# Hybrid decoder step on one core: the first projection of the first 384 tokens taken from x before its norm, and the work around it in another order

## The chip, the core and the metric

The kernel runs on one core of one Trainium2 chip. The core has TensorE (PE in the profile; PEld is its weight load), VectorE (DVE), ScalarE (ACT), GpSimd (POOL) and SyncE (SP), which run side by side and wait for each other through semaphores; SP and ACT also start DMA transfers, each on a queue of its own. The metric is the device time of one execution in microseconds, as the median of several.

## The reference, cut to what matters

One decoder layer for 1024 prompt tokens and 8 x 4 sample tokens (1056 columns together). What the change touches is its very beginning:

```
h = RMSNorm(x)                        # x * rstd(token) * norm1(channel)
proj = h @ w_in                       # z, xBC, dt, u, q, k, v and three gates
u -> S5 branch: a complex diagonal scan over steps, y = Re(C h) + D u
gates = sigmoid(proj[gate columns])   # 3 x 1024 columns
```

rstd is one number for each token, so that x*norm1 @ w, multiplied with rstd afterwards, is the same as h @ w. After this come three mixers, their merging by the gates, an output projection, and the SwiGLU feed-forward part, which are not changed.

## The kernel before, in words

Activations lie transposed: 128 channels on the partitions, tokens along the columns. `HH` and `HL` (8 tiles k of 1056 columns) hold the high and the low half of h in a reduced float format; `WH` and `WL` the same of a weight unit (128 output columns of W, 8 blocks k of 128x128). A product is three matmuls for each k: WH by HL, WL by HH, WH by HH (`mm3`). Tokens are handled in three chunks (`CHUNKS`): 384, 384 and 288 columns, called chunk 0, 1 and 2.

**The u stage.** Weight units 0 to 3 give u. Units 0 and 1 lie in `WRAW`/`WH`/`WL`, 2 and 3 in `WXR`/`WXH`/`WXL`. `u_pair(j, n)` makes units j and j+1 for chunk n, k by k, so that it can follow the arrival of the halves of h; its order is (0,0), (2,0), (0,1), (2,1), (0,2), (2,2), 48 matmuls each. Before a chunk's h can be made, its squares are summed (squares on ACT and DVE, sums of them over k on DVE), the sum over channels taken by `x_sums_pe`, root on ACT (`x_root_act`), reciprocal on DVE (`x_recip_dve`), and the result spread over the partitions by `x_spread_pe`. Then for each k DVE writes x*norm1*rstd (line 702), ACT copies its high half to HH (line 714), and DVE subtracts that to give HL (line 691). For chunk 0 all of this lies ahead of the first `mm3`. ACT casts the first weights to WH by halves of 512 columns (`high_half`), POOL subtracts to give WL (`split_halves`, `split_apart`). ACT copies u from PSUM to `UF` (`evict_u`) and stores it; SP loads it back in another layout (`U`, lines 1063 and 1067) once all four stores have landed.

**The gates.** From unit 4 on PE makes twelve gate units (`gate(g, chunks)`), each with the accumulators `acc[0..2]` for the three chunks. A chunk of tile `no` starts when `acc_free[n]` says that all `no` earlier tiles of that chunk have been evicted; gate 0 is tile 4. ACT evicts each chunk with a tanh into the one buffer `GT` and stores it (line 2330); the next gate's first tanh waits for that store. Between gates PE does small S5 products: `taps(q)` needs `W_re` and `W_im`, which DVE makes from POOL's tables out of six operations of 2048 columns after its last HL (semaphore `w_ok`); `stt_rows(q)` transposes them, ACT evicting; `step_sums` needs U.

All orders are written by hand, one program for each engine. An instruction that waits holds everything behind it on its engine.

Of the kernel before, what the change touches and what calls it, by code (L numbers as in the profile page):

```python
# [9 lines left out]
F32 = mybir.dt.float32  # L10
# [6 lines left out]
P = 128  # L17
# [139 lines left out]
def build(nc, io):  # L157
# [255 lines left out]
    s_xc = [dma_sem("x_chunk1_first"), dma_sem("x_chunk1_last"), dma_sem("x_chunk2")]  # L413
# [6 lines left out]
    first_high, half_ok = sem("first_weights_high"), sem("first_weights_half_split")  # L420
    s_rawx = [dma_sem(f"weights_second_pair{i}") for i in range(2)]
# [47 lines left out]
    s_fst = [Count(s_xc[0], 64), Count(s_xc[1], 64), Count(s_xc[2], 128), Count(s_scv, 16)]  # L469
    s_fop = [Count(s_x[k], 32) for k in range(7)]  # L470
    wt_ok, wh_ok, wl_ok = Count(den_ok, 1), Count(us_ok, 1), Count(ar_ok, 1)
    pd, ar_used, dr = Count(bias_mm, 2), Count(step_ok, 1), Count(sem("quadrant_made"), 0)
    dd, si_ok = Count(den_inv, 1), Count(mag_ok, 1)
    ss_ok, sh_ok, sl_ok = Count(hf_done, 48), Count(h_hi, 48), Count(h_lo, 48)
    fm_ok, fs_ok, fh_ok, fl_ok = Count(sem("ffn_ready"), 0), Count(sem("ffn_sum"), 0), Count(sin_ok, 1), Count(w_ok, 1)
# [3 lines left out]
    h_lo_pool = sem("h_low_by_pool")  # L479
# [110 lines left out]
    def u_bank(j, n):  # L590

        return bank[((0, 1, 2, 3), (4, 6, 7, 0), (1, 2, 3, 4))[n][j]]

    FIRST_SQUARES, FIRST_ADDED = KD // 2, KD + 1
    Y_SQUARES, Y_ADDED = FIRST_SQUARES + 2 * KD, FIRST_ADDED + 2 * KD

    def x_square_at(n, k):

        if n == 0 and k >= 4:
            return ACC[:, 384 * (k - 4):384 * (k - 3)] if k < 6 else HF[k - 6]  # L600
        return SQ[:, k % 4, 0:CHUNKS[n][1]]
# [5 lines left out]
    def x_spread_at(n):  # L607

        return bank[(4, 7, 5)[n]]

    def x_full(i):

        return bank[5 + i % 2] if i < KD else HF[i % 2]

    def x_loaded(n, k):

        return s_x[k] if n == 0 else s_xc[k // 4] if n == 1 else s_xc[2]

    def x_first_square(eng, k):

        eng.wait_ge(x_loaded(0, k), 16)
        if k % 2 == 0:
            nc.scalar.activation(x_square_at(0, k), X0[:, k, 0:384], ACT.Square).then_inc(pq_done, 1)
        else:
            nc.vector.tensor_tensor(x_square_at(0, k), X0[:, k, 0:384], X0[:, k, 0:384], ALU.mult).then_inc(pq_used, 1)

    def x_squares_act(n, ks):
        c0, w = CHUNKS[n]
        base = FIRST_ADDED + KD * (n - 1)
        for k in ks:  # L630
            nc.scalar.wait_ge(x_loaded(n, k), (16, 64, 128)[n])
            if k >= 4 or n == 2:
                nc.scalar.wait_ge(pq_used, base + k - 3)
            nc.scalar.activation(x_square_at(n, k), X0[:, k, c0:c0 + w], ACT.Square).then_inc(pq_done, 1)

    def x_add_dve(n, ks):
        dve = nc.vector
        c0, w = CHUNKS[n]
        for k in ks:
            i = FIRST_ADDED + KD * (n - 1) + k  # L640
            dve.wait_ge(pq_done, FIRST_SQUARES + KD * (n - 1) + k + 1)
            if k == 0:
                dve.tensor_copy(ACC[:, c0:c0 + w], x_square_at(n, k)).then_inc(pq_used, 1)
            else:
                dve.wait_ge(pq_used, i)
                dve.tensor_tensor(ACC[:, c0:c0 + w], ACC[:, c0:c0 + w], x_square_at(n, k), ALU.add).then_inc(pq_used, 1)

    def x_first_sums_pe():

        for k, added in ((1, 2), (3, 4), (7, FIRST_ADDED)):  # L650
            nc.tensor.wait_ge(pq_used, added)
            for j in range(3):
                last = nc.tensor.matmul(x_sums_at(0)[:, j:j + 1], x_square_at(0, k)[:, P * j:P * j + P], prm("ones", 0, 1),
# [40 lines left out]
    def x_split_dve(i0, i1):  # L694
        dve = nc.vector
        for i in range(i0, i1):
# [7 lines left out]
            if k >= 1:  # L704
                x_low_dve(i - 1)
# [3104 lines left out]
```

## Time and profile before

| | us |
|---|---|
| median of 3 runs (1685.58 to 1688.41) | 1686.39 |
| span of the profiled execution | 1684.5 |
| PE busy in it | 1654.0 |
| DVE, POOL, ACT busy | 966.9, 791.2, 556.0 |

The times of runs contain some 2 us ahead of and behind the span. The profile lists work by engine, the line in the kernel and the tiles that an instruction writes and reads (out<-in), with its start and duration. "idle before <-" is how long the engine had stood still and what ended that. The busy share of PE counts matmuls that overlap, so how fast it goes is read from the distance between starts.

### The profile page before, as it was taken

The page shows a single profiled execution, that of the slowest core. Times are in us where ns is not written, and L with a number is a line of the kernel's source. Part 1 is how long each engine was busy: PE and PEld are TensorE (multiplying, and loading weights), DVE is VectorE, ACT ScalarE, POOL GpSimd, SP SyncE. Part 2 cuts the span into 40 slices and gives each one's busy share as a digit, 9 for nine tenths or more (in the row PEclk, how much of TensorE's full clock was granted, in tenths as well). Part 3 has the DMA queues.
Part 4 walks back from the last instruction along what each step waited for, and adds up shares of the span by engine and source line. Part 5 has one row for each costly group of instructions (what it writes and reads, how often), then busy time and mean ns, then how long its engine had stood idle before and what let it go on. Part 6 is the DMA issues. An engine that isn't in the chain of part 4 may idle for free. (4 is left out here: it accounts for less than half of the span.)

```text
span 1684.5 us, 30884 instructions
## 1 busy us (share of the span) xinstructions
PE 1654.0 (98%) x12241; PEld 1604.7 (95%) x12241; DVE 966.9 (57%) x1642; ACT 556.0 (33%) x1240; POOL 791.2 (47%) x756
## 2 busy tenths in 40 slices
PE   7999999999999999999999999999999999999997
PEld 7999999999999998888899999999999999999997
DVE  6859811406634554778873289666665565744346
ACT  5332121342213332543411154443443333322233
POOL 5483122322221111141322325877777777787774
PEclk9999999999999999999999999999999999999998
DMA  5364363232233234434365431543433344966443
GB/s 209 84 127 133 104 203 98 89 92 91 87 93 103 89 130 134 161 115 140 126 218 191 152 126 42 180 162 145 151 141 141 141 167 165 367 224 267 162 187 103
DMA packets 95805, 245.85 MB, mean 146 GB/s; under 512 B 14369, under 2 KB 42273, under 8 KB 95417
## 3 DMA queue, kind: packets, MB, share of 16 engines
q1 hardware_dynamic: 73824, 174.48, 30.5%
q0 software_dynamic: 10256, 33.59, 6.7%
q10 hardware_dynamic: 11592, 35.96, 6.3%
q8 instruction: 90, 1.47, 0.4%
q14 instruction: 43, 0.34, 0.1%
HBM read 177.11 MB, written 66.65 MB: 145 GB/s over the span
## 5 line engine op out<-in xcount | busy, mean ns | idle before, releaser
L1642 PE MATMUL ps<-HL,WH 128*128 128x384 f32 (+1 forms) x1536 | 507.7, 331 | 4.4 <-DVE HL L691 1.8
L1643 PE MATMUL ps<-HH,WL 128*128 128x384 f32 (+1 forms) x1536 | 497.4, 324 | 0.0
L1644 PE MATMUL ps<-HH,WH 128*128 128x384 f32 (+1 forms) x1536 | 496.3, 323 | 0.0
L1642 PEld LDWEIGHTS ps<-HL,WH 128*128 128x128 f32 x1536 | 289.4, 188 | 15.6 <-issue 9.3
L1643 PEld LDWEIGHTS ps<-HH,WL 128*128 128x128 f32 x1536 | 289.7, 189 | 0.3
L1644 PEld LDWEIGHTS ps<-HH,WH 128*128 128x128 f32 x1536 | 289.6, 189 | 0.0
L1285 POOL TENSOR_TENSOR WL<-WRAW,WH 128x1024 fp32r<-128x1024 f32 x59 | 145.0, 2457 | 243.3 <-DMA WH<-in_w 243.3
L1282 POOL DMA_DIRECT2D WH<-in_w x59 | 34.6, 586 | 354.4 <-PE ps L1644 352.9
L2932 DVE TENSOR_TENSOR X<-X,ps 128x528 f32<-128x528 f32 (+2 forms) x170 | 107.9, 656 | 155.5 <-PE ps L2238 104.6
L2327 ACT ACTIVATE GT<-ps 128x384 f32<-128x384 f32 (+1 forms) x72 | 33.4, 465 | 215.5 <-PE ps L1644 183.5
L2932 DVE TENSOR_TENSOR RB<-RB,ps 128x528 f32<-128x528 f32 x60 | 42.1, 701 | 103.4 <-ACT RB L2847 85.9
L1310 POOL TENSOR_TENSOR WRAW<-WRAW 128x512 f32<-128x512 f32 (+2 forms) x72 | 91.8, 1275 | 9.9 <-DVE STG L2932 4.6
L1310 POOL TENSOR_TENSOR RAWB<-RAWB 128x512 f32<-128x512 f32 (+2 forms) x72 | 87.6, 1216 | 5.4
L2236 PE MATMUL ps<-HL,RINGB 128*128 128x264 f32 x272 | 77.4, 285 | 2.1 <-DVE GT L2932 2.1
L2237 PE MATMUL ps<-HH,RINGB 128*128 128x264 f32 x280 | 79.5, 284 | 0.0
L2238 PE MATMUL ps<-HH,RINGB 128*128 128x264 f32 x280 | 79.5, 284 | 0.0
L2236 PE MATMUL ps<-HL,WH 128*128 128x264 f32 x274 | 77.9, 284 | 0.3 <-issue 0.3
L2236 PE MATMUL ps<-HL,WL 128*128 128x264 f32 x270 | 76.6, 284 | 0.0
L2236 PE MATMUL ps<-SOP,RINGB 128*128 128x264 f32 x264 | 75.2, 285 | 0.0
L2237 PE MATMUL ps<-HH,WL 128*128 128x264 f32 x264 | 75.0, 284 | 0.0
L2238 PE MATMUL ps<-SOP,RINGB 128*128 128x264 f32 x264 | 74.9, 284 | 0.0
L2237 PE MATMUL ps<-SOP,RINGB 128*128 128x264 f32 x264 | 74.9, 284 | 0.0
(467 smaller groups left out, 4266.2 us busy)
## 6 DMA issues: line engine op xcount, KB each, us to landing
WRAW<-in_w SPq DMA_DIRECT2D x75, 512.0 KB, 3.4
ffn_scratch<-STG SPq DMA_DIRECT2D x70, 528.0 KB, 3.6
WH<-in_w POOLq DMA_DIRECT2D x62, 512.0 KB, 4.6
SOP<-ffn_scratch SPq DMA_DIRECT2D x36, 528.0 KB, 7.9
gate_scratch<-GT ACTq DMA_DIRECT2D x24, 528.0 KB, 3.2
PX<-gate_scratch ACTq DMA_DIRECT2D x22, 528.0 KB, 4.2
HL<-ffn_scratch SPq DMA_DIRECT2D x22, 528.0 KB, 10.4
RAWB<-in_w SPq DMA_DIRECT2D x10, 1024.0 KB, 6.2
```

The source lines that it names most:

```text
L1282: nc.gpsimd.dma_start(WH[:, slot, 0:wd], src[:, 0:wd]).then_inc(s_high[slot], 16)
L1285: nc.gpsimd.tensor_tensor(WL[:, slot, 0:wd], WRAW[:, slot, 0:wd], WH[:, slot, 0:wd].bitcast(F32), ALU.subtract).then_inc(split_ok, 1)
L1310: return nc.gpsimd.tensor_tensor(out, a, b, op)
L1642: nc.tensor.matmul(out, wh, rl, start=start, stop=False)
L1643: nc.tensor.matmul(out, wl, rh, start=False, stop=False)
L1644: return nc.tensor.matmul(out, wh, rh, start=False, stop=stop)
L2236: nc.tensor.matmul(out, wh, ml, start=product in FRESH and k == 0, stop=False, skip_group_check=True)
L2237: nc.tensor.matmul(out, wl, mh, start=False, stop=False, skip_group_check=True)
L2238: last = nc.tensor.matmul(out, wh, mh, start=False, stop=k == nk - 1, skip_group_check=True)
L2327: nc.scalar.activation(GT[:, c0:c0 + w], acc_of(no, n)[:, 0:w], ACT.Tanh, scale=0.5).then_inc(acc_free[n], 1)
L2932: return nc.vector.tensor_tensor(out, a, b, op)
```

## The change

- **Chunk 0 of u from x without its norm.** ACT writes HH for chunk 0 as the high half of x*norm1 (`x_plain_high_act`), DVE writes HL from that (`x_plain_low_dve`). PE starts `u_pair(0, 0)` from these, behind no sum of squares. rstd of chunk 0 is made later, put in `GT[:, 0:384]`, and DVE multiplies with it when it evicts u of chunk 0 (`evict_first_u_dve`, four of them, formerly ACT copies).
- **The normed h of chunk 0**, which the gates and all later products need, is made last: the order of chunks in `x_split_*` is 1, 2, 0. So PE does gate 0 as chunks 1, 2 and then 0.
- **No wide POOL work in the u stage.** The low halves of weight units 0 to 4 are made by DVE; POOL only counts them and does its S5 tables earlier. The split of unit 5 and later ones stay on POOL.
- **Loads.** Units 0 and 1 come as four half loads on ACT's queue right behind the parameters; SP loads x of chunk 0, units 2 and 3, and then the rest.
- **Squares.** Those of chunks 0 and 1 are added in wide DVE operations; the sum over channels of chunk 0 moves from ahead of the first matmul into `u_pair(0, 1)`, the bias products into `u_pair(2, 0)`.
- **Products with W later.** taps(0) and taps(1) stand behind chunks 0 and 1 of gate 1, formerly behind gate 0's first two chunks; stt_rows(0) and (1) behind chunk 0 of gate 2.
- **ACT** puts the evictions of u between the copies of the split; those of chunk 2 for j = 2 and 3 stand behind the last copy.

```diff
-        return bank[((0, 1, 2, 3), (4, 6, 7, 0), (1, 2, 3, 4))[n][j]]
+        return bank[((0, 1, 2, 3), (4, 5, 6, 7), (1, 2, 3, 4))[n][j]]
+    ROOT_ORDER = (1, 0, 2)
+    SPLIT_ORDER = (1, 2, 0)
+    def x_plain_high_act(k):
+        nc.scalar.wait_ge(s_x[k], 16)
...
+        nc.scalar.mul(HH[:, k, 0:384], X0[:, k, 0:384], prm("norm1", k, 1)).then_inc(xp_hi, 1)
+    def x_plain_low_dve(k):
+        dve.wait_ge(xp_hi, k + 1)
+        dve.scalar_tensor_tensor(HL[:, k, 0:384], X0[:, k, 0:384], prm("norm1", k, 1), HH[:, k, 0:384].bitcast(F32),
+                                 ALU.mult, ALU.subtract).then_inc(xp_lo, 1)
+    def x_root_copy_act():
+        nc.scalar.wait_ge(pn_rs, 2)
+        nc.scalar.copy(GT[:, 0:384], x_spread_at(0)[:, 0:384]).then_inc(r0_ok, 1)
+    def evict_first_u_dve(j):
+        dve.wait_ge(r0_ok, 1)
+        dve.wait_ge(acc_done[0], j + 1)
+        dve.tensor_tensor(as_steps(UF[:, j, :], 0, 3), as_blocks(u_bank(j, 0), 3), as_blocks(GT[:, 0:384], 3),
+                          ALU.mult).then_inc(acc_free[0], 1)
# PE, u stage
-        x_first_sums_pe()
-        bias_by_distance(0)
-        bias_by_distance(1)
-        x_spread_pe(0)
         u_pair(0, 0)
-        pe.wait_ge(bias_ev, 2)
-        u_pair(2, 0, {1: lambda: x_sums_pe(1), 3: lambda: x_spread_pe(1)})
-        u_pair(0, 1)
-        u_pair(2, 1, {1: lambda: x_sums_pe(2), 3: lambda: x_spread_pe(2)})
+        u_pair(2, 0, {1: lambda: bias_by_distance(0), 2: lambda: bias_by_distance(1), 3: lambda: x_sums_pe(1),
+                      5: lambda: x_spread_pe(1)})
+        u_pair(0, 1, {1: lambda: x_sums_pe(0), 5: lambda: x_spread_pe(0)})
+        u_pair(2, 1, {2: lambda: x_sums_pe(2), 4: lambda: x_spread_pe(2)})
         u_pair(0, 2)
         u_pair(2, 2)
# PE, gates
-        gate(0, [0, 1])
+        gate(0, [1, 2])
+        gate(0, [0], lambda n, k: pe.wait_ge(h_lo, 2 * KD + k + 1))
+        gate(1, [0, 1])
         taps(0)
-        gate(0, [2])
         taps(1)
-        gate(1, [0])
+        gate(1, [2])
         taps(2)
-        gate(1, [1])
         taps(3)
-        gate(1, [2])
+        gate(2, [0])
         stt_rows(0)
-        for n in range(3):
-            gate(2, [n])
-            stt_rows(n + 1)
+        stt_rows(1)
+        gate(2, [1])
+        stt_rows(2)
+        gate(2, [2])
+        stt_rows(3)
# ACT, behind chunk 0
+        evict_u(0, 1)
+        evict_u(1, 1)
+        x_root_act(2)
+        x_split_act(8, 12)
+        evict_u(2, 1)
+        x_split_act(12, 14)
+        evict_u(3, 1)
+        x_split_act(14, 18)
+        evict_u(0, 2)
+        x_split_act(18, 19)
+        high_weights(4)
+        x_split_act(19, 20)
+        evict_u(1, 2)
+        x_split_act(20, 22)
+        high_weights(5)
+        x_split_act(22, 24)
         for j in range(4):
-            evict_u(j, 2)
-            if j == 1:
-                high_weights(4)
-                high_weights(5)
+            if j >= 2:
+                evict_u(j, 2)
+            act.wait_ge(acc_free[0], j + 1)
             act.wait_ge(acc_free[2], j + 1)
             act.dma_start(uscr[j * P:(j + 1) * P, :], UF[:, j, :]).then_inc(s_ust, 16)
# DVE, behind chunk 1
+        x_split_dve(4, 8)
+        x_third_sum_dve()
+        for j in range(3):
+            evict_first_u_dve(j)
         x_recip_dve(2)
-        x_split_dve(16, 24)
+        evict_first_u_dve(3)
+        x_split_dve(8, 20)
+        dve.wait_ge(first_high, 7)
+        tt(high_low(4)[1], WRAW[:, 0, :], high_low(4)[0].bitcast(F32), ALU.subtract).then_inc(half_ok, 1)
+        x_split_dve(20, 24)
```

ACT from its first instruction on, before; the names are the tiles written and read (SP is the table of S5 parameters, SQ, ACC and HF take squares of x, X is x as loaded):

```order
L2332 DMA PRM<-in_params 128x428
L2334 ACT_TABLE_LOAD
L2334 ACTIVATE SP<-ZERO 128x1
L2336 ACTIVATE SP<-PRM 128x16
L2338 ACTIVATE SP<-SP 128x16
L623 ACTIVATE SQ<-X 128x384 x2
L623 ACTIVATE ACC<-X 128x384
L623 ACTIVATE HF<-X 128x384
L2410 ACT_TABLE_LOAD
L2410 ACTIVATE SP<-ZERO 128x1
L2355 CAST WH<-WRAW 128x512 x2
```

and in the changed kernel:

```order
L2368 DMA PRM<-in_params 128x428
L2372 DMA WRAW<-in_w 128x512 x4
L2374 ACT_TABLE_LOAD
L2374 ACTIVATE SP<-ZERO 128x1
L2376 ACTIVATE SP<-PRM 128x16
L634 ACTIVATE HH<-X,PRM 128x384
L2448 ACTIVATE SP<-SP 128x16
L2393 CAST WH<-WRAW 128x512 x2
L634 ACTIVATE HH<-X,PRM 128x384 x3
L2393 CAST WH<-WRAW 128x512 x2
```

Four loads stand ahead of the first table load, and the first HH stands where squares stood.

DVE from its first instruction on in the changed kernel (UF and GT hold squares here; before it began with squares of x too, and its first HL was its twelfth operation):

```order
L640 SCALAR_TENSOR_TENSOR HL<-X,PRM,HH 128x384
L2977 TENSOR_TENSOR WL<-WRAW,WH 128x512 x2
L640 SCALAR_TENSOR_TENSOR HL<-X,PRM,HH 128x384 x3
L2977 TENSOR_TENSOR WL<-WRAW,WH 128x512 x2
L640 SCALAR_TENSOR_TENSOR HL<-X,PRM,HH 128x384 x4
L2977 TENSOR_TENSOR WXL<-WXR,WXH 128x1024 x2
L3017 RECIPROCAL SP<-SP 128x16
L651 TENSOR_TENSOR UF<-X 128x768
L677 TENSOR_TENSOR GT<-X 128x768
```

The weights' low halves, which were POOL's, stand between the low halves of x.

ACT at the end of the u stage, before (UF takes u, of which the 128x2x8x16 and 128x32 are chunk 2; WH of units 4 and 5):

```order
L714 CAST HH<-HF 128x288 x8
L2398 COPY UF<-ps 128x3x8x16 x2
L2398 COPY UF<-ps 128x2x8x16
L2400 COPY UF<-ps 128x32
L2453 DMA u_scratch<-UF 128x1056
L2398 COPY UF<-ps 128x2x8x16
L2400 COPY UF<-ps 128x32
L2348 CAST WH<-WRAW 128x1024 x2
L2453 DMA u_scratch<-UF 128x1056
```

and in the changed kernel:

```order
L2436 COPY UF<-ps 128x2x8x16
L2438 COPY UF<-ps 128x32
L779 CAST HH<-HF 128x384 x2
L2386 CAST WH<-WRAW 128x1024
L779 CAST HH<-HF 128x384 x2
L2496 DMA u_scratch<-UF 128x1056 x2
L2436 COPY UF<-ps 128x2x8x16
L2438 COPY UF<-ps 128x32
L2496 DMA u_scratch<-UF 128x1056
```

The stores of u and the evictions of its last two tiles stand behind the last copies of chunk 0's split, which come after those of chunk 2.

## Rows read from the trace of the kernel before

**Rows 1.** The page: the span, and PE's busy time, share and instructions.
```profile
span 1684.5 us, 30884 instructions
PE 1654.0 (98%) x12241; PEld 1604.7 (95%) x12241; DVE 966.9 (57%) x1642; ACT 556.0 (33%) x1240; POOL 791.2 (47%) x756
```
**Rows 2.** Waits of PE in the first 120 us: us in total, times, longest.
```profile
PE ps L653 <- DVE SQ L2932: 6.2, 1, 6.2
PE ps L1642 <- DVE HL L691: 1.8, 1, 1.8
```
**Rows 3.** Busy time of PE in stretches of the u stage (x matmuls), clock, DMA, GB/s.
```profile
17.30:21.00 3.70, 3.70 (x12) 1.00 1.08 368
21.00:27.30 6.30, 6.30 (x37) 1.00 0.83 315
```
**Rows 4.** Timeline of PE: start, us; where the u pairs and gate 0 begin.
```profile
17.30 0.69 PE L1642 MATMUL ps<-HL,WH 128*128 128x384 f32 x1 [1.82 <-DVE HL L691]
...
27.51 0.34 PE L1642 MATMUL ps<-HL,WXH 128*128 128x384 f32 x1
...
37.71 0.34 PE L1642 MATMUL ps<-HL,WH 128*128 128x384 f32 x1
...
46.11 0.34 PE L1642 MATMUL ps<-HL,WXH 128*128 128x384 f32 x1
...
56.12 0.29 PE L1642 MATMUL ps<-HL,WH 128*128 128x288 f32 x1
...
69.16 0.41 PE L1642 MATMUL ps<-HL,WH 128*128 128x384 f32 x1
```
**Rows 5.** Timeline of the start: parameters' arrival on ACT, DMA in one microsecond, bias products.
```profile
4.22 0.22 ACT L2336 ACTIVATE SP<-PRM 128x16 f32<-128x16 f32 x1 [1.38 <-DMA PRM<-in_params]
...
5.00:6.00 1.00, 0.00 (x0) 0.00 (x0) 0.77 (x2) 0.89 (x3) 0.83 (x3) 1.00 1.06 381
...
11.86 1.05 PE L1745 MATMUL ps<-HOT,RTAB 33*8 33x264 f32 x4
```
**Rows 6.** Timelines of ACT and DVE: weight casts, and h of chunk 1.
```profile
13.47 1.12 ACT L2355 CAST WH<-WRAW 128x512 fp32r<-128x512 f32 x2
...
36.75 0.61 DVE L702 SCALAR_TENSOR_TENSOR HF<-X,PRM,ps 128x384 f32<-128x384 f32 x1
37.28 0.56 DVE L691 TENSOR_TENSOR HL<-HF,HH 128x384 fp32r<-128x384 f32 x1
37.94 0.61 DVE L702 SCALAR_TENSOR_TENSOR HF<-X,PRM,ps 128x384 f32<-128x384 f32 x1
```
**Rows 7.** Timeline of ACT: eviction and store of u, tanh of gate 0's first chunk.
```profile
62.29 0.37 ACT L2398 COPY UF<-ps 128x256 f32<-128x256 f32 x1 [2.10 <-PE ps L1644]
62.56 0.19 ACT L2400 COPY UF<-ps 128x32 f32<-128x32 f32 x1
62.78 0.34 ACTq L2453 DMA_DIRECT2D u_scratch<-UF  x1
...
73.65 0.49 ACT L2327 ACTIVATE GT<-ps 128x384 f32<-128x384 f32 x1 [1.99 <-PE ps L1644]
```
**Rows 8.** Timelines of DVE (products for W) and of POOL (split of unit 4).
```profile
64.36 2.29 DVE L2932 TENSOR_TENSOR W_re<-W_re,KTS 128x2048 f32<-128x2048 f32 x1
66.69 4.36 DVE L2932 TENSOR_TENSOR W_im<-PWD,BC 128x2048 f32<-128x2048 f32 x1
...
75.48 2.29 DVE L2932 TENSOR_TENSOR W_im<-W_im,KTS 128x2048 f32<-128x2048 f32 x1
...
64.66 4.24 POOL L1487 TENSOR_TENSOR WL<-WRAW,WH 128x1024 fp32r<-128x1024 f32 x1 [9.78 <-ACT WH L2348]
```
**Rows 9.** Timelines of SP and ACT: U's first loads, gate 1's tanh, unit 7's cast.
```profile
76.56 9.19 SPq L1063 DMA_DIRECT2D U<-u_scratch  x8
...
97.51 0.87 ACT L2327 ACTIVATE GT<-ps 128x384 f32<-128x384 f32 x2 [12.35 <-DMA gate_scratch<-GT]
...
101.10 1.05 ACT L2348 CAST WH<-WRAW 128x1024 fp32r<-128x1024 f32 x1 [0.53 <-DMA WRAW<-in_w]
```

More of the change, by code:

```diff
@@ new lines, in x_first_squares_act, with x_first_rest_dve, x_first_add_dve @@
+    def x_first_squares_act(ks):
+        for k in ks:
+            nc.scalar.activation(SQ0[:, k, :], X0[:, k, 0:384], ACT.Square).then_inc(pq_done, 1)
+    def x_first_rest_dve():
+        dve, rest = nc.vector, slice(FIRST_BY_ACT, KD)
+        dve.tensor_tensor(SQ0[:, rest], X0[:, rest, 0:384], X0[:, rest, 0:384], ALU.mult).then_inc(x0_add, 1)
+    def x_first_add_dve(i):
+        dve = nc.vector
+        if i == 0:
+            dve.wait_ge(pq_done, FIRST_BY_ACT)
+        dve.wait_ge(x0_add, i + 1)
+        if i < 2:
+            n = 4 >> i
+            dve.tensor_tensor(SQ0[:, 0:n], SQ0[:, 0:n], SQ0[:, n:2 * n], ALU.add).then_inc(x0_add, 1)
@@ L648, in x_first_sums_pe, with x_second_sum_dve @@
[L648 to L653, printed above, removed]
-                                        start=(k == 1 and j == 0), stop=k == KD - 1, skip_group_check=True)
-        last.then_inc(pn_sum, 1)
-    def x_sums_pe(n):
-        nc.tensor.wait_ge(pq_used, FIRST_ADDED + KD * n)
+    def x_second_sum_dve():
+        dve, pairs = nc.vector, GT[:, 0:768].rearrange("p (k c) -> p k c", c=384)
+        dve.wait_ge(s_xc[1], 128)
+        dve.tensor_tensor(pairs, X0[:, 6:8, 384:768], X0[:, 6:8, 384:768], ALU.mult).then_inc(pq_used, 1)
+        dve.wait_ge(pq_done, FIRST_BY_ACT + 4)
+        dve.tensor_tensor(SQ[:, 0:2], SQ[:, 0:2], SQ[:, 2:4], ALU.add).then_inc(pq_used, 1)
+        dve.wait_ge(pq_used, 2)
+        dve.tensor_tensor(SQ[:, 0:2], SQ[:, 0:2], pairs, ALU.add).then_inc(pq_used, 1)
+        dve.wait_ge(pq_done, FIRST_BY_ACT + SECOND_BY_ACT)
+        dve.wait_ge(pq_used, 3)
+        dve.tensor_tensor(SQ[:, 0:2], SQ[:, 0:2], HF0[:], ALU.add).then_inc(pq_used, 1)
+        dve.wait_ge(pq_used, 4)
+        dve.tensor_tensor(ACC[:, 384:768], SQ[:, 0], SQ[:, 1], ALU.add).then_inc(pq_used, 1)
@@ L1541, in _ @@
                 split_apart(6)
-                s5_squarings(0)
                 s5_squarings(1)
@@ L1672, in unit, with gate @@
         def unit(u, slot, tiles):
-            pe.wait_ge(split_ok, u + 1)
+            pe.wait_ge(*((half_ok, 7) if isinstance(u, int) and u == UNIT0["gates1"] else (split_ok, u + 1)))
             for args, kw in tiles:
                 tile(args[0], slot, *args[1:], **kw)
-        def gate(g, chunks=range(3)):
+        def gate(g, chunks=range(3), before=None):
             u = (UNIT0["gates1"] + g) if g < 12 else (UNIT0["gates2"] + g - 12)
             no = (TILE0["gates1"] + g) if g < 12 else (TILE0["gates2"] + g - 12)
-            unit(u, u % 2, [((no, 0, KD, HH, HL), dict(chunks=chunks))])
+            unit(u, u % 2, [((no, 0, KD, HH, HL), dict(chunks=chunks, before=before))])
         def simple_loop(name, pairs, nk, RH, RL, skip=0, kbase=0, before=None):
@@ L2332, in _ @@
         act.dma_start(PRM[:, 0:NPAR_FIRST], io["params"][:, 0:NPAR_FIRST]).then_inc(s_par, 16)
+        for half in range(2):
+            c = slice(512 * half, 512 * half + 512)
+            for u in range(2):
+                act.dma_start(WRAW[:, u, c], io["w"][u][:, c]).then_inc(s_half0 if half == 0 else s_raw[u], 16)
         act.wait_ge(consts_ok, 1)
@@ L2494, in _ @@
         high_weights(7)
+        gate(2, [0])
         stt_rows(0)
-        for n in range(3):
-            gate(2, [n])
-            stt_rows(n + 1)
+        stt_rows(1)
+        gate(2, [1])
+        stt_rows(2)
+        gate(2, [2])
+        stt_rows(3)
         u_sample_copy()
```

288 lines of the change are left out of this document (140 added, 148 removed).

## The prediction, made before the changed kernel was run

> **What bounds the kernel now.** I read the page first: PE is busy for 1654.0 of 1684.5 us [rows 1], so only time in which PE stands still or runs slowly can be won. PE's waits give it: 6.2 us for the first squares and 1.8 us for the first low half HL are the largest of the first 120 us, and both lie ahead of the first projection matmul [rows 2]. That matmul starts at 17.30 us [rows 4]. What PE did before it is small sums and spreads. From there PE is never behind anything for long: 48 matmuls of 384 columns take 46.11 - 37.71 = 8.4 us, 0.175 us each, the 96 of 288 columns 69.16 - 56.12 = 13.0 us, 0.136 each [rows 4]. The first twelve are slow: 3.70 us for 12, then 6.30 us for 37, which is 0.31 and 0.17 us each, near 1.2 and then 2.4 GHz, though the granted clock reads 1.00 in both rows [rows 3]. So the prize is the start at 17.30, and whatever PE reaches earlier must be ready earlier too.
>
> **The new start.** Ahead of the first matmul now stand: half 0 of units 0 and 1 in WRAW, two casts on ACT, and on DVE the low half of x tile 0 and of both weight halves. The loads: the parameters (214 KB) came at 4.2 us, and DMA moves 381 KB in a microsecond [rows 5]. By the order of issue the second half-0 load has about 1.33 MB ahead of or in it (parameters, three tiles of x at 197 KB, two halves at 262 KB), 3.5 us at that rate; from a first byte at 2.5 us (4.2 less the time of parameters and two x tiles) and half a microsecond for the landing this is 6.5 us. The casts take 1.12 us for two [rows 6]. DVE's operation with 512 columns is bounded by 0.56 us for 384 [rows 6] and 2.29 for 2048 [rows 8], that is 0.16 us and 1.04 ns a column: 0.7 us, of which the second stands behind the second cast. 6.5 + 1.1 + 0.7 and some 0.3 for three handings-over: PE starts at 8.6 us, 8.7 earlier. The ends are 8.0 and 9.6. The Trainium skill ("DMA: Bandwidth & Descriptors", Arbitration) says that each DMA engine takes turns between its queues by packets. Then ACT's 0.74 MB would go at half the rate and land at 6.9 instead of 6.5 us; no row here shows two full queues side by side, and the sum goes without it.
>
> The twelve slow matmuls stay, since PE is as idle before as it was: no gain, no loss. Within u_pair(0,0) x tiles come every 0.5 us and ACT and DVE take 1.1 us for a tile's halves side by side; PE needs 1.05 us for a k at full speed, and 1.9 at first. I count no wait there. Units 2 and 3 need two DVE operations of 1.2 us (1024 columns), done at about 17 us, and PE is there at 18.8.
>
> **What moves behind the start.** The two bias products were hidden in PE's idle time (1.05 us at the slow rate [rows 5]); now they cost 0.5. So were the sums and spread of chunk 0: chunk 1's cost 37.71 - 27.51 - 8.4 = 1.8 us [rows 4], and chunk 0's will cost the same. Chunk 1's h: DVE makes a tile in 37.94 - 36.75 = 1.19 us [rows 6], PE uses one in 1.05. Before, PE never waited for it. Now the spread of chunk 1 ends only two k, 2.1 us, ahead of u_pair(0,1), and DVE needs 1.8 us from there to the first HL (twice 0.61 and 0.56). Between tiles 3 and 4 stands the reciprocal of chunk 0 (it waits for PE's sums and a root on ACT), and ahead of the copy of tile 7 stands ACT's copy of the spread of chunk 0, which is issued behind k = 5 on PE. Followed step by step, PE waits 0.2 to 0.3 us at k = 4 and 5 and 0.55 at k = 7: 0.85 together. The ends are 0.3 and 2. u_pair(2,1) and the pairs of chunk 2 I find just covered: DVE's last low half comes 8.5 us after the spread of chunk 2, PE wants it after 8.75.
> So gate 0 starts 8.7 - 0.5 - 1.8 - 0.85 = 5.55 us earlier, at 63.6.
>
> **The gates.** ACT's evictions of u, chunk 2, for j = 2 and 3 now stand behind its last copy for chunk 0. DVE splits chunk 0 after chunk 2, eight tiles of 1.19 us and unit 4's low half (1.2); its last tile but one is given to ACT about 2.3 us after PE's last u matmul. Behind that ACT does two stores and an eviction, a store, an eviction (0.34 and 0.56 us [rows 7]): the fourth is free some 4.5 us after gate 0's start. Gate 0's second chunk wants it after 4.2. **0.3 us**. Chunk 0 of gate 1 follows directly on chunk 0 of gate 0 with the same accumulator, and must wait for a tanh: 0.49 us [rows 7] and two handings-over. **0.75 us**; before, another chunk always lay between.
>
> W: DVE's six operations of 2.29 us make 13.75. DVE ends its splits some 5 us after gate 0's start, later by POOL's split of unit 5 (2.2 us, below) and of unit 6 within the products. w_ok is due at 63.6 + 5 + 2.2 - 1 + 13.75 + 2.2, about 85 us (it was 75.48 + 2.29 = 77.8 [rows 8]). PE is at taps(0) after 5 chunks of gates: 63.6 + 4 x 4.2 + 3.3 + 0.3 + 0.75 = 84.8. No wait of weight, by 0 to 1 us. Before, it was as near: w_ok at 77.8, with gate 0's two chunks done at 77.6. The order of the products a gate later costs nothing in itself: it is what PE needs as DVE's work ends later while PE comes earlier.
>
> At stt_rows(0) and (1), which now stand together behind gate 2's first chunk, the second pair of transposes waits for ACT to do the tanh and the first copy. **0.4 us**. Later stages depend on PE's own results (S5 rotations wait for the transposes) and move along. POOL's squarings come earlier, which shortens DVE's rotations, but PE did not wait for these: nothing.
>
> The sum: 5.55 - 0.3 - 0.75 - 0.4 = **4.1 us**. The profiled span of 1684.5 becomes 1680.4, and with the same 1.9 us around it the median becomes **1682.3 us**.
>
> **A rule against it.** With POOL's split of unit 4 asked for at 64.66 us, DVE's running operation took 2.29 us and its next one 4.36, and POOL's own 4.24 [rows 8]: one went wholly ahead of the other, each losing some 2.1 us. The Trainium skill ("SBUF — State Buffer", Who interferes with whom) says that a DVE instruction with two inputs in SBUF and a GpSimd one that reads SBUF share a port pair as an exclusive lock. The trace agrees. Unit 5's split remains on POOL and becomes ready when DVE is about to start its last multiplication for chunk 0, which has two SBUF inputs now (X and GT, formerly PSUM). By my walk DVE starts that one 0.1 us ahead of POOL. If POOL is first, ACT's last copy comes 2.2 us later and so do the evictions behind it.
>
> **Rivals.**
> POOL first: gate 0's second chunk waits 2.5 us, not 0.3. For it: the tie above. Against: POOL has a semaphore more to pass. It gives 4.1 - 2.2 = 1.9 us, **1684.5**.
>
> The load of U takes a time that does not move. It starts when all four stores of u have landed, 76.56 us [rows 9], 7.4 after gate 0's start. Now the stores are issued from 65.5 to 68; their 2.2 MB take 5.7 us at 381 KB in a microsecond [rows 5], so U's loads start at 73 to 75 though PE is 4 to 5 us further. Gate 0's store lay among them and landed at 97.51, 21 us after their start, and unit 7's weights were there at 101 [rows 9]. In the new order ACT casts unit 7 ahead of gate 2's first tanh. My sum takes gate 0's store as early in the queue, landed by 90, and unit 7 at 98.5, in time. If instead that store lands 21 us after U's start again, gate 2 (due at 94.5) waits for gate 1's tanh to about 98, and gate 1's store and unit 7 hold ACT until 102 to 104, so that the transposes wait 2 us too: 3.4 + 2.1 - 0.4 = 5.1 us more. That ends 1 us slower than before, **1687.4**. It decides from the point where gate 0's store lands after 94.5 us.
>
> All is hidden: DVE keeps up and none of the four waits occurs: 8.7 - 0.5 - 1.8 = 6.4, **1680.0**. Against it is that two of the waits (the tanh, the tile supply) follow from durations of rows.
>
> The change doesn't do what it says at the start: the halves of W, four loads on a second queue beside x, land as late as before, when two of the first casts still ran from 13.47 [rows 6], or ACT's four issues and table load push x tile 0 out. Half 0 at 9.4 instead of 6.5: 4.1 - 2.9 = 1.2 us, **1685.2**.
>
> **How the numbers follow.** I give my sum 0.50, POOL first 0.18, U's load 0.10, all hidden 0.12, late weights 0.10. A measurement of this kernel tells some 0.2% from no change, 3.4 us. Faster by more than that needs below 1683.0: nearly all of my sum's own case (0.44, the rest of it for an error of 0.8 us), all of "all hidden", little else: 0.57. Slower by more needs above 1689.8, which only U's load reaches, with more waits behind it, or a thing I don't see: 0.05. Within: 0.38. The range of 8 in 10 leaves out U's load and a little at the lower end: 1680.2 to 1686.3.
>
> **What would show it.** PE's first projection matmul at 8.0 to 9.6 us, and twelve slow ones behind it. u_pair(0,1) 9.7 us after the sums and 0.85 of waits in it. Gate 0 at 63.6. A wait of PE for ACT's UF (0.3, or 2.5 if POOL was first, seen in DVE's last line of chunk 0 at over 2 us), one for ACT's tanh of 0.75 directly behind gate 0, w_ok near 85. Wrong would be: any wait of PE above 1 us in gates 1 and 2 (then U's load or W decides), a PE clock that falls back after such a wait, or a first matmul after 10 us.

## The result, and the profile after

The changed kernel takes **1688.08 us** (median of 20 runs, 1684.27 to 1694.42); the kernel before 1685.93 beside it (20 runs, 1684.25 to 1688.41). The ratio is 1.0014, 95% interval 1.0008 to 1.0020: no gain, and by the interval a small loss of 2.2 us. The prediction had a gain of 4.1 us and put 1682.3; 1688.08 lies above its range, too. The profiled execution took 1685.05 us, with a span of 1683.3. That is 3 us under the median, which matters below.

The page, answering to [rows 1]: PE has 12 instructions and 3.4 us of busy time less.

```profile
span 1683.3 us, 30854 instructions
PE 1650.6 (98%) x12229; PEld 1599.4 (95%) x12229; DVE 976.5 (58%) x1650; ACT 556.8 (33%) x1244; POOL 790.3 (47%) x749
```

Waits of PE in the first 120 us, which answer to [rows 2] (us in total, times, longest):

```profile
PE ps L1680 <- DVE WL L2977: 8.8, 1, 8.8
PE ps L1680 <- ACT UF L2438: 1.9, 1, 1.9
PE ps L1680 <- DVE HL L752: 0.9, 1, 0.9
PE ps L1680 <- ACT GT L2363: 0.7, 1, 0.7
PE ps L1842 <- ACT STT L2500: 0.2, 1, 0.2
PE ps L709 <- DVE ACC L697: 0.2, 1, 0.2
```

The waits of the prediction for a tile, for UF, for the tanh and for STT are there; the one for UF is six times as long as its sum had it. PE's timeline, answering to [rows 4] (start, duration, line, operation, count, idle time before it and what ended that):

```profile
8.82 0.66 PE L1680 MATMUL ps<-HL,WH 128*128 128x384 f32 x1 [8.82 <-DVE WL L2977]
...
18.66 0.34 PE L1680 MATMUL ps<-HL,WXH 128*128 128x384 f32 x1
...
29.87 0.40 PE L1680 MATMUL ps<-HL,WH 128*128 128x384 f32 x1
...
41.40 0.34 PE L1680 MATMUL ps<-HL,WXH 128*128 128x384 f32 x1
...
64.67 0.34 PE L1680 MATMUL ps<-HL,WH 128*128 128x384 f32 x1
...
70.93 0.40 PE L1680 MATMUL ps<-HL,WH 128*128 128x288 f32 x1 [1.88 <-ACT UF L2438]
...
79.27 0.42 PE L1680 MATMUL ps<-HL,WH 128*128 128x384 f32 x1 [0.67 <-ACT GT L2363]
...
87.78 0.30 PE L1827 MATMUL ps<-CDG,W_re 128*128 128x32 f32 x2
```

Read it against [rows 4]: the first projection matmul starts at 8.82 instead of 17.30, 8.5 us earlier. Gate 0 starts at 64.67 instead of 69.16, 4.5 us earlier. A mark behind all moved work is the first matmul of step_sums with KTS, here of before and of after (min/median/max ns, first and last start in us):

```profile
L1844 PE MATMUL ps<-U,KTS x64: 277/279/385, 151.9 to 228.0; 128*128 128x137 f32 x64
```
```profile
L1878 PE MATMUL ps<-U,KTS x64: 277/279/386, 150.6 to 226.7; 128*128 128x137 f32 x64
```

So 8.5 us at the start are 4.5 at gate 0 and **1.3 us** at KTS. Two losses are to be found. A third one isn't in this record at all: with 1.3 us gained, the median would be 1684.6 (1685.93 − 1.3), and it is 3.5 us above that. One record can be luckier than the median, so the next question is what other records of the same kernel show.

### The profile page after: what moved, and what is told of

The parts are those of the page before. It is cut to its first block and busy times, and to the rows that moved or that the text cites. A ratio compares the mean times of both kernels' runs of the same rounds, so it can differ in the third digit from the quotient of the medians.

```text
span 1683.3 us, 30854 instructions
## 1 busy us (share of the span) xinstructions
PE 1650.6 (98%) x12229; PEld 1599.4 (95%) x12229; DVE 976.5 (58%) x1650; ACT 556.8 (33%) x1244; POOL 790.3 (47%) x749
```

## The experiments

Each ratio is against the kernel before, run beside it on the same chip; it is not the quotient of the two medians, and where the two disagree (before_stall, four_taps, best2) the text gives both. The record of before, and that of the changed kernel shown above, have no fall in this stretch, and KTS at 151.9 and 150.6. "Falls" are stretches of 4 us between 30 and 160 us of the record with a granted clock under 1.00.

| Run | Median us (before) | Ratio, interval | KTS at us | Falls |
|---|---|---|---|---|
| same_a, the changed kernel again | 1687.79 (1686.03) | 1.0012, 1.0003–1.0020 | 153.0 | 72 |
| same_b, again, one execution | 1690.87 | – | 157.4 | 72, 92 to 108 |
| evict_first | 1685.45 (1686.03) | 0.9999, 0.9989–1.0009 | 150.9 | 88 to 96 |
| late_start | 1693.99 (1686.03) | 1.0045, 1.0032–1.0058 | 164.3 | 80, 104 to 116 |
| before_pairs | 1686.99 (1686.02) | 1.0006, 0.9997–1.0015 | 151.3 | none |
| apart | 1686.84 (1686.02) | 1.0007, 0.9998–1.0016 | 150.9 | none |
| evict_apart | 1684.07 (1686.02) | 0.9987, 0.9978–0.9996 | 148.5 | none |
| best | 1683.41 (1686.02) | 0.9984, 0.9975–0.9993 | 147.2 | none |
| before_stall | 1690.29 (1686.11) | 1.0017, 1.0007–1.0026 | 154.8 | 72 to 80 |
| best2 | 1682.31 (1686.11) | 0.9972, 0.9961–0.9983 | 146.8 | none |
| best_b, best again, one execution | 1686.16 | – | 147.7 | none |
| before_b, before again, one execution | 1686.37 | – | 151.5 | none |
| evict_b, evict_first again | 1685.94 (1686.08) | 1.0003, 0.9993–1.0013 | 149.3 | none |
| four_taps | 1689.63 (1686.08) | 1.0016, 1.0007–1.0025 | 153.9 | 92 to 104 |
| evict_apart_b, evict_apart again | 1684.72 (1686.08) | 0.9991, 0.9982–1.0001 | 148.5 | none |

### The changed kernel again: same_a, same_b

> The changed kernel once more, unchanged. Its first profile ran 1.2 us shorter than the one of before, with PE starting at 8.82 us and 1.88 us of waiting for the evictions of u, while the median of its 20 runs was 2.2 us longer and the longest 8 us longer, those runs with a lower mean granted clock (0.991 to 0.993 against 0.996). Theory A (clock): the same spread again, 1684 to 1694, and runs with a lower clock are the longer ones; their trace, where one is caught, has the u stage as in the first profile and more stretches at half clock than the one or two of before. Theory B (the waits differ from run to run): the clock is the same in all, and a long run's trace has PE waits above those 3.5 us in total in the first 120 us.

> The changed kernel again for a second trace. Theory A: if this run is long, half-clock stretches account for the length; if it is short, 1683 to 1685 with at most one stretch.

The loss repeats: 1687.79, ratio 1.0012. And the two records show where the time beyond the waits is. PE in stretches of 4 us, first of the record of after, then of same_a, then of same_b (length, PE busy with the number of matmuls, granted clock, DMA share, GB/s):

```profile
68.00:72.00 4.00, 2.12 (x14) 1.00 0.65 259
72.00:76.00 4.00, 4.00 (x29) 1.00 0.71 282
```
```profile
68.00:72.00 4.00, 2.15 (x13) 1.00 0.42 172
72.00:76.00 4.00, 4.00 (x20) 0.57 0.94 369
```
```profile
72.00:76.00 4.00, 4.00 (x21) 0.57 0.87 342
76.00:80.00 4.00, 4.00 (x25) 1.00 0.87 104
...
92.00:96.00 4.00, 4.00 (x24) 0.61 1.23 172
96.00:100.00 4.00, 4.00 (x20) 0.54 0.89 144
100.00:104.00 4.00, 4.00 (x33) 0.89 0.36 136
104.00:108.00 4.00, 4.00 (x18) 0.69 0.00 0
```

In all three PE has just stood still for 1.9 us (busy 2.1 of 4.0 in 68 to 72). In two of the three the clock then reads 0.57 for the next 4 us: it is at its lower level, 1.2 GHz, for most of them, and 20 matmuls are issued instead of 29. PE is "busy" for the whole 4.00 us in both cases, so neither the waits nor the busy time tell of it; the granted clock and the count do. At 4 us times 0.43 this costs 1.7 us. same_b has a second fall from 92 on, worth 1.6 + 1.8 + 0.4 + 1.2 = 5.1 us (rounded last). With the 1.7 these are the 6.8 us by which its KTS is behind that of after (157.4 and 150.6). What stands there are the taps, which the change has put together in twos; PE's timeline in same_b at the end of the first two and at the end of the next two:

```profile
92.51 0.39 PE L1827 MATMUL ps<-CDG,W_re 128*128 128x32 f32 x2
92.73 0.52 PE L1827 MATMUL ps<-CDG,W_im 128*128 128x32 f32 x2
93.06 0.61 PE L1827 MATMUL ps<-CDG,W_re 128*128 128x32 f32 x2
...
102.81 0.39 PE L1827 MATMUL ps<-CDG,W_re 128*128 128x32 f32 x2
103.03 0.58 PE L1827 MATMUL ps<-CDG,W_im 128*128 128x32 f32 x2
```

Both times the products go slow (0.39 to 0.61 us for the same two) at the end of a row, the first begun at 89.92 and the second at 99.77, without any wait there. So there were two suspects: the wait at gate 0, and the rows of small products. The rivals: that the falls are chance, that they belong to this stage whatever stands in it, or that the early start of PE brings them. The rival of same_a's expectation, that PE's waits differ from run to run, is out: the waits of the three records agree within 0.4 us each (the start within 0.8), and their KTS lies 6.8 us apart.

### The wait at gate 0: evict_first, before_stall

The wait is the prediction's rival "POOL first". DVE and POOL in the record of after:

```profile
66.01 2.53 DVE L767 SCALAR_TENSOR_TENSOR HF<-X,PRM,GT 128x384 f32<-128x384 f32 x1
```
```profile
65.63 2.49 POOL L1526 TENSOR_TENSOR WL<-WRAW,WH 128x1024 fp32r<-128x1024 f32 x1
```

POOL's split of unit 5 begins 0.4 us ahead of DVE's last multiplication for chunk 0. That one then shows 2.53 us where its forerunner took 0.62, and the two end within 0.4 us of each other. It was no accident of one execution: in all 13 records with the changed order POOL begins 0.37 to 0.39 us ahead, and DVE's operation takes 2.53 to 2.55 us. ACT stands until 68.58 for it, and the stores and evictions follow, the second eviction ending at 70.87:

```profile
68.58 0.51 ACT L779 CAST HH<-HF 128x384 fp32r<-128x384 f32 x1 [2.61 <-DVE HF L767]
68.64 0.83 ACTq L2496 DMA_DIRECT2D u_scratch<-UF  x2
69.50 0.37 ACT L2436 COPY UF<-ps 128x256 f32<-128x256 f32 x1 [0.42 <-issue]
```

The experiment takes the evictions (2,2) and (3,2) from behind the last cast and the stores, so that they no longer stand behind the cast that waits for this operation:

```diff
         high_weights(5)
+        evict_u(2, 2)
+        evict_u(3, 2)
         x_split_act(22, 24)
         for j in range(4):
-            if j >= 2:
-                evict_u(j, 2)
             act.wait_ge(acc_free[0], j + 1)
```

> The changed kernel with ACT's evictions of u, chunk 2, for j = 2 and 3 ahead of the last two copies of chunk 0's split instead of behind them and two stores. Both theories: PE's wait of 1.88 us at gate 0 goes. W's last product still ends near 85.3 us and gate 1's taps stand behind it, so that some 0.5 us of the 1.88 may come back as a wait for W: 1.4 to 1.9 us shorter in the profile. Theory A with waits of PE as the cause of the clock's falls: the spread over runs shrinks as well and the median falls by 3 us or more. Theory A with another cause: the median falls by 1.4 to 1.9 us and the spread stays.

The wait is gone from PE's list and nothing takes its place, though POOL still goes first here (66.48 against 66.87, and 2.55 us for DVE's operation). So it is the order on ACT that turned that delay into a wait of PE:

```profile
PE ps L1680 <- DVE WL L2977: 9.2, 1, 9.2
PE ps L1680 <- ACT GT L2363: 0.7, 1, 0.7
PE ps L1680 <- DVE HL L752: 0.5, 1, 0.5
PE ps L1842 <- ACT STT L2500: 0.2, 1, 0.2
```

The median falls from 1687.79 to 1685.45, by 2.3 us for a wait of 1.9, and the spread of its runs does not shrink (7.0 us against 5.4). KTS of this record is no earlier than that of after, since it has a fall at 88 to 96 us (1.7 us); evict_b, the same kernel without a fall, has 149.3. That doesn't tell the cost of the clock by itself. So the wait was put where there had been none, into the kernel before, ahead of gate 0's chunk 1 (the fifth of DVE's six operations for W):

```diff
-        gate(0, [0, 1])
+        gate(0, [0])
+        pe.wait_ge(chain, 5)
+        gate(0, [1])
         taps(0)
```

> The kernel before, whose TensorE now waits between gate 0's chunk 0 and chunk 1 for VectorE's fifth operation for W, about 75.4 us where the chunk would start at 73.5: a wait of 1.9 us at the place where the changed kernel has one of 1.9. taps(0) then come at 79.8 instead of 77.9. If a wait costs its own length alone, the median rises by 1.9 us, to 1687.9 (ratio 1.0011). If TensorE's clock falls behind such a wait, as it did in two records of the changed kernel of three, it rises by 2.5 to 3.6 us (ratio 1.0015 to 1.0021), and the record can show a stretch near 0.57 at 76:80 us.

Measured: 1690.29 beside 1686.11, 4.2 us between the medians. The ratio, 1.0017, makes it **2.9 us** (interval 1.2 to 4.4), which is what was expected if the clock falls; its interval doesn't exclude the 1.9 us of the wait alone. What decides is the record. The timeline of PE at the wait, and the two stretches that hold it:

```profile
75.02 0.44 PE L1642 MATMUL ps<-HL,WH 128*128 128x384 f32 x1 [1.90 <-DVE KTS L2934]
...
75.47 0.48 PE L1644 MATMUL ps<-HH,WH 128*128 128x384 f32 x1
75.75 0.52 PE L1642 MATMUL ps<-HL,WH 128*128 128x384 f32 x1
```
```profile
72.00:76.00 4.00, 2.10 (x11) 0.94 0.64 257
76.00:80.00 4.00, 4.00 (x17) 0.64 0.81 98
```

The first matmuls behind the wait are still quick; from 75.47 on they are slow, 0.52 instead of 0.34 us each. At KTS this record stands at 154.8, 2.9 us behind the record of before and 3.3 behind that of before_b: the 1.9 us of the wait, and 1.0 to 1.4 of clock. A wait of 1.9 us followed by half the speed is thus shown, in one record, in a kernel that has nothing else of the change, and the 2.9 to 3.3 us at KTS agree with the 2.9 of the ratio. The record has falls at 388, 772 and 1056 us as well, 1.7 us each, at places that this edit doesn't touch (more on them at the end).

### The small products in a row: before_pairs, apart, evict_apart, four_taps

```diff
         gate(0, [0, 1])
         taps(0)
-        gate(0, [2])
         taps(1)
+        gate(0, [2])
         gate(1, [0])
         taps(2)
-        gate(1, [1])
         taps(3)
+        gate(1, [1])
```

> The kernel before with its taps put in twos: taps(0), taps(1) one behind the other after gate 0's first two chunks, taps(2), taps(3) after gate 1's first, some 3.5 us of small products in a row where there were 1.8; nothing else is changed. If the small products in a row bring TensorE's clock down to its lower level by themselves, the median rises by 1 to 4 us (ratio 1.0005 to 1.0025), and the record shows a stretch of a granted clock under 0.9 near 80 to 110 us in part of the executions. If only the long wait at gate 0 does it, the ratio is 1.000 within 0.0005 and the clock stays at 1.00 there. Something of it can be a wait instead: taps(1) a gate chunk earlier can meet W_im's last flag.

1686.99 beside 1686.02: 1.0 us, with an interval on both sides of 1.000, and a record without a fall, the fastest of its eleven runs. Nothing decided. The other way round, in the changed kernel (apart) and with the evictions of evict_first (evict_apart), no two of them stand together on PE (ACT's order of step transposes follows):

```diff
+        def halfway(step):
+            return lambda n, k: step() if k == 4 else None
+
         gate(1, [0, 1])
         taps(0)
-        taps(1)
         gate(1, [2])
-        taps(2)
+        taps(1)
+        gate(2, [0], halfway(lambda: taps(2)))
         taps(3)
-        gate(2, [0])
-        stt_rows(0)
+        gate(2, [1], halfway(lambda: stt_rows(0)))
         stt_rows(1)
-        gate(2, [1])
-        stt_rows(2)
-        gate(2, [2])
+        gate(2, [2], halfway(lambda: stt_rows(2)))
         stt_rows(3)
```

> The changed kernel with its taps and step transposes spread out on TensorE: no two of them one behind the other, two set halfway into a gate chunk. The wait of 1.9 us at gate 0 stays. If the clock falls in the grouped small products, this takes about 1.5 us off the median (1686.3 where the changed kernel has 1687.9) and the stretches under 0.9 at 84 to 110 us are gone, while one at 72:76 may stay. If the wait alone does it, nothing changes: 1687.9, within 0.4.

> Both edits: ScalarE evicts (2,2) and (3,2) of u ahead of its last quarter of the casts, and the small products are spread out. If both causes count, the record shows no stretch under 0.9 between 30 and 1660 us, the median is 1684 (1683.2 to 1684.8, ratio 0.9982 to 0.9994) and the spread of its runs shrinks to that of the kernel before. If the grouped products don't matter, 1685.4 as with the evictions alone.

apart has 1686.84, evict_apart 1684.07: 1.0 and 1.4 us less than the kernels with twos (same_a, evict_first, on another chip). The record of apart has the wait of 1.9 us at gate 0 and no fall behind it. evict_apart missed one of its signs: its record has a fall at 380 to 388 us, where none was expected from 30 us on. The intervals with and without twos overlap, so it was asked again, side by side on one chip, with the row doubled as the third case:

```diff
         gate(1, [0, 1])
+        gate(1, [2])
         taps(0)
         taps(1)
-        gate(1, [2])
         taps(2)
         taps(3)
```

> The two evictions ahead of the last casts, as run before, beside the two kernels that follow: 1685.5 (1684.9 to 1686.1). The taps stand in twos.

> The same with all four taps in one row behind gate 1's last chunk: 7 us of products of 32 columns where there were two rows of 3.5. If small products in a row bring the clock down, the median is 1 to 3 us above that of the two rows (1686.5 to 1688.5) and the record shows a granted clock under 0.8 right at their end, at 92 to 100 us. If the number in a row doesn't matter, 1685.5 within 0.5 and no fall there beyond what the two rows show.

> The same with the taps and step transposes spread out, as run before (1684.1 then): 1 to 1.8 us under the one with two rows if small products in a row count, the record without a fall between 60 and 150 us; the same as it within 0.4 if not.

No row 1684.72, two rows of two 1685.94, one row of four **1689.63**. Twice the row costs 3.7 us by the medians and 2.2 by the ratios (1.0016 and 1.0003, whose intervals overlap), where 1 to 3 were expected. None of it is a wait: the waits of the two records are the same four, within 0.1 us behind the start. PE's timeline of four_taps, and its stretches:

```profile
92.53 0.45 PE L1827 MATMUL ps<-CDG,W_re 128*128 128x32 f32 x2
92.79 0.62 PE L1827 MATMUL ps<-CDG,W_im 128*128 128x32 f32 x2
```
```profile
92.00:96.00 4.00, 4.00 (x25) 0.59 1.26 122
96.00:100.00 4.00, 4.00 (x20) 0.50 0.98 248
100.00:104.00 4.00, 4.00 (x17) 0.63 0.00 0
```

The row begins at 89.49, its products are slow from 92.79 on, and the clock stays at its lower level beyond the end of the row. In KTS this is 153.9 against 149.3. Against the kernel with no row the intervals lie apart (1.0007 to 1.0025, and 0.9982 to 1.0001). So the row of four is shown to bring the clock down; the edit also moves the first two taps behind one more chunk, and how much of the cost that place has wasn't separated. For rows of two the sign is the same in each comparison (1.2, 1.4, 1.0 and, put into the kernel before, 1.0 us), and the records go with it: a fall in or right behind the rows in three of the seven records that have them (same_b, evict_first, late_start), in none of the six with the products spread and none of three of the kernel before's order. Each interval by itself still touches the other, so for two it is likely, not shown.

### The early start by itself: late_start

PE waits for all six splits of units 0 to 3 ahead of u_pair(0, 0); the rest is as in the changed kernel:

```diff
+        pe.wait_ge(half_ok, 6)
         u_pair(0, 0)
```

> The changed kernel with PE's first projection matmul held until all six low halves of weights 0 to 3 are there (16.0 us instead of 8.82). All that is after it in the u stage is then bounded by PE, and the waits for tile supply (0.9) and W go or shrink. By the sum of the prediction it costs 7.2 us less 1 to 3 us of waits that vanish: 4 to 6 us longer in the profile than the changed kernel. If the early start, with PE busy beside a loading DMA and full DVE and ACT, is what brings the clock down, its mean clock returns to 0.996 and its spread to that of before (4 us), and the median is then no worse than the changed kernel's.

The first matmul is at 16.7 us, near where it was before [rows 4], and the median at 1693.99, 6.2 above the changed kernel and **8.0 us above the kernel before**, though PE starts 0.6 us ahead of it. That splits the change in two: the early start is worth 6.2 us, and the order that it needs (with the sums and bias products of chunk 0 that now stand behind the start) costs 8.0. It also answers the rival of the early start: with a late one the falls are still there and the median is longer, not shorter. The record is that of the slowest of its five runs (1698.77; the others 1693.3 to 1694.0). It has the wait for UF at gate 0 (1.8 us), with a clock of 0.58 in the 4 us behind it, and 0.50 and 0.66 at 108 to 116, behind the taps.

### Two waits less: best, best2

On top of evict_apart's edits:

```diff
-        gate(1, [0, 1])
+        gate(1, [1, 0])
...
-            if k == 6:
+            if k == 7:
                 x_root_copy_act()
...
-        gate(1)
+        gate(1, [1, 0, 2])
```

> The same with two more waits taken out: gate 1 takes chunk 1 ahead of chunk 0 on TensorE and ScalarE (the 0.7 us for tanh of gate 0's chunk 0), and ScalarE's copy of the root norm stands behind its cast of k 7 (the 0.9 us wait for a tile's halves). Expected 1.6 us under the kernel before it in this list, less what moves elsewhere: 1682.8 (1682 to 1684), ratio 0.998, which would be faster than both kernels. If the time goes by the last supply of a product in each case, one of the two comes back as a wait of the next tile, and it is 1683.5.

Both waits (0.7 for tanh, 0.5 to 0.9 for a tile) went; PE was early enough to wait 0.8 us for W ahead of taps(0), and the median was 1683.41, where 1682.8 was expected, or 1683.5 if one of the waits came back. best_b has another record of it:

> A second record of the kernel with all four edits: first group with KTS at 147.2 us on TensorE if the clock stays up. It was then 4.7 us earlier than before there, and only 2.6 in the median: if the rest is clock, this record or the timed runs show a stretch under 0.9 between 60 and 150 us, or near 385 us, worth 1.5 us each; if the rest is in what follows, the way from there to the end is longer than before's with the clock at 1.00.

No fall between 60 and 150 us; but falls at 380, 764 and 1048 us, and 1686.16. What best lost between KTS and the end in that execution was clock, at places far from the change. For the wait for W, taps(0) went half a chunk further back:

```diff
         gate(1, [1, 0])
-        taps(0)
-        gate(1, [2])
+        gate(1, [2], halfway(lambda: taps(0)))
         taps(1)
```

> The kernel of the last batch with all four edits, its taps(0) half a gate chunk later: W_im was ready 0.8 us after TensorE stood ready for taps(0). Expected: that wait of 0.8 us gone and nothing in its place, 1682.6 (ratio 0.998) where the other had 1683.4; if the time goes by something behind it, 1683.4 again.

PE's waits in the first 120 us of best2, whole:

```profile
PE ps L1680 <- DVE WL L2976: 9.4, 1, 9.4
```

There is none but the start. KTS is at 146.8, 5.1 us ahead of before. **1682.31 us** beside 1686.11, ratio 0.9972, interval 0.9961 to 0.9983: 3.8 us faster than before by the medians, 4.7 by the ratio, and 5.8 faster than the changed kernel (measured at different times, the kernel before 1686.11 and 1685.93 beside them).

### The kernel before again: before_b

> A second record of the kernel before, unchanged: KTS at 151.9 us. Its first record had a stretch at 0.79 at 384:392 us, which four of nine others had too. If that comes by chance in each execution, this record has it or not, and the span goes with it by 1.6 us: 1682.9 or 1684.5.

No fall near 385, and yet a span of 1684.7: this record waits once for 1.5 us more for POOL's WL at 240 us. The expectation that the span follows that one fall is wrong. Each of these two records of the kernel before has lost some 1.5 us, at different places.

## Why the prediction was wrong

Its sum against the first record (us earlier; minus is a loss):

| Step | Predicted | Record of after |
|---|---|---|
| First matmul (17.30 to 8.82) | 8.7 | 8.5 |
| Slow matmuls at the start: first pair 9.84 instead of 10.21 | 0 | +0.4 |
| Bias products, 20.85 to 21.39 and 22.64 to 23.18 | −0.5 | −1.1 |
| Sums and spread of chunk 0, 0.6 each | −1.8 | −1.2 |
| Tile supply in u_pair(0, 1): 11.53 − 8.40 − 1.17 | −0.85 | −2.0 |
| Gate 0 starts (the rows leave 0.1 over) | 5.55 | 4.5 |
| Evictions at gate 0 | −0.3 | −1.9 |
| Tanh ahead of gate 1 | −0.75 | −0.7 |
| STT copies | −0.4 | −0.2 |
| KTS (the rows leave 0.4 over) | 4.1 | 1.3 |
| From this record to the median: clock ahead of KTS in others, and what stays open | 0 | −3.5 |

**The start** was right within 0.2 us: the rival of late weights did not occur, and neither did that of U's load. Gate 0's store did land late, ACT stood 11.89 us for it up to 92.52 and 4.81 us for unit 7 up to 99.96, yet PE waited for neither. ACT's timeline, answering to [rows 9]:

```profile
92.52 0.87 ACT L2363 ACTIVATE GT<-ps 128x384 f32<-128x384 f32 x2 [11.89 <-DMA gate_scratch<-GT]
...
99.96 1.05 ACT L2386 CAST WH<-WRAW 128x1024 fp32r<-128x1024 f32 x1 [4.81 <-DMA WRAW<-in_w]
```

DVE's last operation for W ended at 85.34 (80.97 and 4.37; predicted 85), PE came to the taps at 87.78: no wait. The terms that the prediction writes down for it add up to 85.75, not to 85, which against its 84.8 for PE would have been a wait of 1 us; it went well because PE came 3 us later than forecast. The bias products were mis-sized by halving their 1.05 us for the clock: at a granted clock of 1.00 they take 0.54 each, as long as at the slow rate.

**Tile supply** was mis-sized, but by less than its row says: 48 matmuls with their sums and spread take 11.53 us (29.87 to 41.40), where 8.40 [rows 4] and 1.17 for the small ones would do. Only 0.9 of the 2.0 us appear as a wait, at the last tile; the rest are gaps of a tenth or two between matmuls, which no list of waits shows and the row of one pair against another does. The prediction's 1.8 for the sums was read as such a distance (10.2 − 8.4) and holds the gaps around them. So the two rows belong together: 2.65 us forecast, 3.1 measured.

**The evictions** are the first step that failed. It said "By my walk DVE starts that one 0.1 us ahead of POOL". POOL began at 65.63, DVE at 66.01. A tie of 0.1 us, in a walk whose other steps were off by 0.2 to 1 us, was no ground for 0.3 against 2.5 us. And it is no tie: POOL is first in every record. The rival "POOL first", to which the prediction gave 0.18, is what happened here, with 1.9 us for its 2.5. With 1.6 us more here the forecast was already at 1684, still inside its range.

**The clock** is the step that put it outside. "Wrong would be: ... a PE clock that falls back after such a wait" names it, but the sum carried no term for it, and no rival had it as a price. It has two sources. The clock falls behind the longer wait in three of the five records that have it at gate 0 (same_a, same_b, late_start; not after, apart); that the wait is the cause is shown by before_stall, in a kernel without the change. And "The order of the products a gate later costs nothing in itself" is wrong: the step put taps in twos, and small products in a row bring the clock down without a wait (shown for four, 2.2 to 3.7 us beyond two twos; likely for two, 1.0 to 1.4). What the lower level costs stood in [rows 3]: 0.31 us for a matmul instead of 0.17.

**What the 3.5 us are.** They are counted from a record without a fall. In the three records of the changed kernel falls cost 0, 1.7 and 6.8 us ahead of KTS, 2.8 in the mean, and KTS is at 153.7 in the mean, 2.0 us behind the kernel before (151.9, 151.5), where the medians are 2.2 apart. Three records are few, but they leave little of the loss to be looked for behind KTS. With both sources taken out the loss is gone: evict_apart is at 0.9987 (0.9978 to 0.9996) where same_a is at 1.0012 (1.0003 to 1.0020).

**What stays open** is a part of the gain. evict_apart has KTS 3.4 us ahead of before and the median 1.9 and 1.4; best has 4.7 and 2.6, best2 5.1 and 3.8. So 1.3 to 2 us are lost behind KTS, where the code is the same. Some 0.9 of them is a wait of PE at about 1055 us. Here is the line of the page that has it, of before and of after (busy us, mean ns, then the idle time ahead of the group and what ended it):

```profile
L2236 PE MATMUL ps<-SOP,WH 128*128 128x264 f32 x246 | 69.9, 284 | 0.7 <-DVE RB L2932 0.7
```
```profile
L2272 PE MATMUL ps<-SOP,WH 128*128 128x264 f32 x246 | 70.0, 284 | 1.8 <-DVE RB L2977 1.8
```

PE waits there for 0.7, 0.9 and 1.1 us in before, before_b and before_pairs, and for 1.5 to 2.0 in ten of the records with the changed order; the others have 0.6 (late_start), or a fall right ahead of it and 0.2 or none. Why DVE's result comes later there wasn't followed. For the rest, best_b shows falls at 380, 764 and 1048 us; whether they come more often than in the kernel before, these records are too few to tell.

The Trainium skill ("TensorE: Matmul & The Clock Gate", HAM oscillation) describes kernels whose matmuls come in short bursts between waits and run at half speed each time. The records here agree as to the wait, in a part of the executions (0.57 behind 1.9 us in three of five). For rows of small products without a wait only the runs here speak.

## What to carry to other kernels

Where a change makes PE stand for a microsecond or two, or lines up its smallest products, price the clock beside the wait: some 1.7 us for each fall, in part of the executions. Look for it in the granted clock and the number of matmuls of short stretches, in more than one record: the first one here had no fall where two others had. Spread small products between large ones, and put an engine's short releases (here two evictions) ahead of a job that waits for an operation which another engine can hold up (here 2.53 us instead of 0.62). Where two engines reach such a place almost together, price the worse order.

## What the runs showed of the hardware

- The clock fell inside an unbroken row of products with 32 columns, while PE counts as busy throughout: two of them took 0.61 us instead of 0.39. Nothing of this stands in the list of waits or in the busy time.
- The nine slow matmuls at the start (8.82 to 11.83, 0.33 us each) show a granted clock of 1.00, while each later fall shows 0.5 to 0.9. At the start the column doesn't show it.
- Whether a fall occurs is settled anew in each execution, and where it can occur is not chance. Of 17 records, whose code from 160 us on does the same, ten have one to three falls between there and 1660 us, 16 in all, 1.6 us each where the marks on either side can be compared: from KTS to the first matmul with PX and PU (674.7 us in the record of before), before needs 522.8 us with a fall at 384 and the changed kernel 521.1 without. Each of the 16 begins within 2 us behind one of the two things that the experiments found; this is read from the records and no run tested it at these places. Six stand behind a wait of PE of 1.8 to 2.1 us (near 695, 1048 and 1058 us). Ten stand behind a row of small products without a wait: eight near 385 us behind 18 products of 8 columns that take 2.0 us, two near 768 us behind 3 us of small S5 products. The row near 385 us in late_start, and PE behind it:

```profile
395.96 1.95 PE L1953 MATMUL ps<-PRM,DTF 16*128 16x8 f32 x16
397.84 0.22 PE L1954 MATMUL ps<-PRM,DTF 16*32 16x8 f32 x2
...
398.44 0.52 PE L1681 MATMUL ps<-HH,WL 128*128 128x384 f32 x1
```

  The same waits and rows stand in the records without a fall too (the row near 385 us is followed by one in 8 of 17). No run here tells what decides it.
